# Recurrent stage of a two-layer trunk: three changes of instruction order, and two of eight output tiles finished on VectorE

## What is computed

```
for i in range(2):
    hn = rmsnorm(x, mix_pre_g[i])
    y  = pool_mixer(hn, ...) if i == 0 else mlstm_mixer(hn, ...)
    x  = x + rmsnorm(y, mix_post_g[i])
    hn = rmsnorm(x, ffn_pre_g[i])
    y  = square(relu(hn @ w1[i])) @ w2[i]
    x  = x + rmsnorm(y, ffn_post_g[i])
```

## Time and profile before

| | |
|---|---|
| median of 3 runs | 1971.12 us (1970.82 to 1972.35) |
| the profiled execution's own time | 1969.38 us |
| its span, first to last instruction | 1967.6 us |
| mean granted clock of TensorE | 0.999 |
| PE busy | 1932.8 us, 98% |
| DVE busy | 1321.8 us, 67% |
| ACT busy | 1064.2 us, 54% |
| POOL busy | 91.0 us, 5% |

### The profile page before, as it was taken

The page is one execution under the profiler, slowest core; times in us unless marked ns, Lnnn a source line. Parts: engine busy times, 40 slices in busy tenths (PEclk is TensorE's granted clock), DMA queues, the critical chain, the costliest instruction groups (busy, mean ns, idle before and its releaser), DMA issues. The chain is left out here.

```text
span 1967.6 us, 24435 instructions
## 1 busy us (share of the span) xinstructions
PE 1932.8 (98%) x8582; PEld 1546.2 (79%) x8582; DVE 1321.8 (67%) x2070; ACT 1064.2 (54%) x1803; POOL 91.0 (5%) x121
## 2 busy tenths in 40 slices
PE   9999999999999999999999999899999999999999
PEld 6678888888788788878878878777888888878786
DVE  5775656565678877776866857776656565577864
ACT  7645454554445446766756757544554545445433
POOL 0110000000000100110000100021000000000110
PEclk9999999999999999999999999999999999999999
DMA  5344234348633533343223442243524344853353
GB/s 213 103 157 177 103 136 161 134 177 297 229 94 103 197 111 100 118 150 97 97 77 104 135 135 96 66 150 119 191 91 163 132 165 172 315 186 97 112 196 115
DMA packets 80568, 283.94 MB, mean 144 GB/s; under 512 B 9504, under 2 KB 9632, under 8 KB 73536
## 3 DMA queue, kind: packets, MB, share of 16 engines
q1 hardware_dynamic: 64576, 237.86, 34.6%
q0 software_dynamic: 8320, 27.27, 4.3%
q10 hardware_dynamic: 7552, 17.26, 2.7%
HBM read 213.08 MB, written 69.27 MB: 144 GB/s over the span
## 5 line engine op out<-in xcount | busy, mean ns | idle before, releaser
L1807 DVE TENSOR_TENSOR w_lo<-raw,w_hi 128x1024 fp32r<-128x1024 f32 x148 | 185.8, 1256 | 188.5 <-ACT w_hi L1266 185.4
L1266 ACT CAST w_hi<-raw 128x1024 fp32r<-128x1024 f32 x148 | 154.3, 1042 | 195.7 <-PE core L1006 54.1
L787 PE MATMUL bank<-x_hi,w_hi 128*128 128x512 f32 x560 | 227.4, 406 | 7.0 <-issue 6.6
L1452 ACT CAST h_hi<-h_raw 128x512 fp32r<-128x512 f32 x178 | 110.3, 620 | 222.6 <-PE core L1006 137.5
L789 PE MATMUL bank<-x_hi,w_lo 128*128 128x512 f32 x560 | 221.7, 396 | 0.0
L788 PE MATMUL bank<-x_lo,w_hi 128*128 128x512 f32 x560 | 220.6, 394 | 0.0
L2062 DVE TENSOR_TENSOR h_lo<-h_raw,h_hi 128x512 fp32r<-128x512 f32 x178 | 122.9, 690 | 106.9 <-ACT h_hi L1452 106.5
L1004 PE MATMUL core<-h_hi,w_hi 128*128 128x512 f32 x448 | 177.9, 397 | 2.5 <-ACT w_hi L1468 2.5
L1006 PE MATMUL core<-h_hi,w_lo 128*128 128x512 f32 x448 | 176.8, 395 | 0.0
L1005 PE MATMUL core<-h_lo,w_hi 128*128 128x512 f32 x448 | 176.5, 394 | 0.0
L1956 DVE TENSOR_TENSOR w_lo<-sums,w_hi 128x512 fp32r<-128x512 f32 x96 | 66.3, 691 | 99.7 <-ACT w_hi L1294 97.1
(11 more groups left out here) (333 smaller groups left out, 4444.2 us busy)
## 6 DMA issues: line engine op xcount, KB each, us to landing
raw<-weights SPq DMA_DIRECT2D x148, 512.0 KB, 3.3
h_pair_dram<-y SPq DMA_DIRECT2D x24, 1792.0 KB, 6.6
h_raw<-h_pair_dram SPq DMA_DIRECT2D x168, 256.0 KB, 2.8
w<-second_pairs SPq DMA_DIRECT2D x32, 768.0 KB, 4.5
x_scratch<-y POOLq DMA_DIRECT2D x48, 256.0 KB, 2.6
raw_odd<-first_pairs SPq DMA_DIRECT2D x12, 1024.0 KB, 7.1
raw<-first_pairs SPq DMA_DIRECT2D x12, 1024.0 KB, 7.1
xold<-x_scratch POOLq DMA_DIRECT2D x40, 256.0 KB, 3.8
```

The source lines that it names most:

```text
L787: nc.tensor.matmul(o, a, hi(t), start=(k == 0), stop=False)
L1266: nc.scalar.copy(w_hi[:, ROW[u] * T:(ROW[u] + 2) * T], raw[:, (n % RAW) * BLK:(n % RAW + 1) * BLK]).then_inc(hi_ready, 1)
L1452: nc.scalar.copy(h_slot(n)[0], h_raw[:, at % H_RAW, :]).then_inc(h_hi_ready, 1)
L1807: dve.tensor_tensor(w_lo[:, s], raw[:, (n % RAW) * BLK:(n % RAW + 1) * BLK], w_hi[:, s].bitcast(F32), ALU.subtract).then_inc(lo_ready, 1)
```

## The change

It has four parts.

1. In every round j from 1 to 15, `split_hi` and `split_lo` of the fourth weight block move ahead of `tick(j, 1)`, on ACT and on DVE.
2. In rounds 4, 8 and 12 (`j % FT == 0`) DVE does `gate_head(j-1)` ahead of `tick(j, 2)` and not behind it. In round 8 that tick is empty.
3. After the last head ACT computes `decay_matrix` ahead of `by_tokens`.
4. At the end, tiles 3 and 7 leave PE and ACT: DVE adds the old input itself, directly into the tile that is stored.

```
+END_ADDED = (3, 7)
...
             for k in range(KT):
-                sp.wait_ge(end_taken, k + 1)
+                if k in END_ADDED:
+                    sp.wait_ge(end_added, END_ADDED.index(k) + 1)
+                else:
+                    sp.wait_ge(end_taken, k + 1 - sum(a < k for a in END_ADDED))
                 sp.dma_start(out[1, k], end_sq[:, k, :]).then_inc(out_stored[1], 16)
...
-            for k in range(KT):
-                if k == KT - 1:
-                    pe.wait_ge(std_ready, NORMS)
+            tiles = [k for k in range(KT) if k not in END_ADDED]
+            for k in tiles:
                 nc.tensor.matmul(last_bank(k)[:, :], ident, x_last[:, k, :], start=True, stop=False)
...
                         tick(j - 1, 3)
+                        decay_matrix(j - 1)
                         by_tokens(j - 1)
-                        decay_matrix(j - 1)
...
                         rows_to_all(j)
+                    split_hi(BLOCK["head", j, 2] + 1)
                     tick(j, 1)
-
-                    split_hi(BLOCK["head", j, 2] + 1)
                     conv_input(j, 1)
...
                     states(j - 1)
+                    split_lo(BLOCK["head", j, 2] + 1)
                     tick(j, 1)
-                    split_lo(BLOCK["head", j, 2] + 1)
                     conv(j, 1)
...
+                    if j % FT == 0:
+                        gate_head(j - 1)
                     tick(j, 2)
-                    gate_head(j - 1)
+                    if j % FT:
+                        gate_head(j - 1)
...
+                scaled = normed(dve, y[1][:, k, :], y[1][:, k, :], CHAINS[-1][1] + k)
+                if k not in END_ADDED:
+                    scaled.then_inc(end_scaled, 1)
+                    continue
+                steps.finish(scaled)
+                dve.wait_ge(x_last_landed, 16)
+                dve.tensor_tensor(end_sq[:, k, :], x_last[:, k, :], y[1][:, k, :], ALU.add).then_inc(end_added, 1)
```

More of the change, by code:

```diff
@@ L411, in build @@
         end_taken = sem("last_output_taken")
+        end_added = sem("last_residual_added")
         x_first_landed = sem("first_old_x_landed")
@@ L1177, in _ @@
             pe.wait_ge(y_added, 2 * ADDS)
-            for k in range(KT):
-                if k == KT - 1:
-                    pe.wait_ge(std_ready, NORMS)
+            tiles = [k for k in range(KT) if k not in END_ADDED]
+            for k in tiles:
                 nc.tensor.matmul(last_bank(k)[:, :], ident, x_last[:, k, :], start=True, stop=False)
-            for k in range(KT):
-                pe.wait_ge(end_scaled, k + 1)
+            for at, k in enumerate(tiles):
+                pe.wait_ge(end_scaled, at + 1)
                 nc.tensor.matmul(last_bank(k)[:, :], ident, y[1][:, k, :], start=False, stop=True).then_inc(end_done, 1)
@@ L1789, in _ @@
             root(norms.pop(0))
-            for k in range(KT):
-                act.wait_ge(end_done, k + 1)
+            for at, k in enumerate(k for k in range(KT) if k not in END_ADDED):
+                act.wait_ge(end_done, at + 1)
                 nc.scalar.copy(end_sq[:, k, :], last_bank(k)[:, :]).then_inc(end_taken, 1)
@@ L2424, in _ @@
             for k in range(KT):
-                normed(dve, y[1][:, k, :], y[1][:, k, :], CHAINS[-1][1] + k).then_inc(end_scaled, 1)
+                scaled = normed(dve, y[1][:, k, :], y[1][:, k, :], CHAINS[-1][1] + k)
[5 more added lines that the diff above has]
+                dve.tensor_tensor(end_sq[:, k, :], x_last[:, k, :], y[1][:, k, :], ALU.add).then_inc(end_added, 1)
 def kernel(x, mix_pre_g, mix_post_g, ffn_pre_g, ffn_post_g, pool_w, pool_b, pool_scale,
```

## The result

| | before | changed |
|---|---|---|
| median | 1970.97 us (8 runs, 1969.66 to 1972.35) | 1977.65 us (8 runs, 1976.60 to 1979.53) |
| the profiled execution's own time | 1969.38 | 1976.84 |
| its span | 1967.6 | 1975.0 |
| mean granted clock in it | 0.999 | 0.995 |

The ratio is 1.0036, with a 95% interval of 1.0026 to 1.0046: slower by 6.7 us. The forecast was 1974.5, with 1968.0 to 1977.5 as its range, and no measurable change as its verdict. The median lies 0.15 above the range, and the slowdown is clear.

A forecast was written before the change was run, and what follows sets the result against it. PE, busy 98%, was taken as the bound, waiting on DVE in rounds 2, 4, 10 and 12. 2 x (2.3 + 0.9) + 1.35 + 1.0 - 3.35 - 2.0 = +3.4 took 1971.12 to 1974.5 us; range 1968.0 to 1977.5.

The forecast's parts named there:

- rival B: Fourth blocks: the splits were all that PE waited for; -13.3 us in all, 1957.8; chance 0.07.
- about 3: Sign in rounds 2, 4, 10 and 12: PE idle about 3 us before `turn_back`, no pause at the fourth block.
- a late second block: Round 4, output product: with part 2, PE starts the second block at 877.7, before 876.35; the round costs +1.35.
- A DVE instruction with two SBUF inputs is held until 2.1 us into the reduction: Rule for DVE under POOL's reduction, read from two rows and applied to the convolution in rounds 2 and 10.
- the 2.3 a round: Rounds 2 and 10: convolution held under the reduction until 807.29 for 804.99, +2.3 us in each.
- a held convolution: Rounds 2 and 10: the convolution's three instructions read two SBUF tiles and are held by the reduction, +2.3 us each.
- its bound of 2.5: Rounds 2 and 10: upper bound of part 1's cost, 2.5 us, if the two small copies are held too.
- The step that failed: the clock: Half clock behind PE's pauses: 0.9 us each in rounds 2 and 10, nothing added in rounds 4 and 12.
- rival C: Rounds 2 and 10: the half clock costs its full 1.7; +5.0 us in all, 1976.1; chance 0.24.
- the cover: Rounds 4 and 12: the late second output block covers the lost clock, so the half clock costs nothing there.
- 1.02: Rounds 4 and 12, part 1: the convolution starts 1.02 us later, and `hnorm` and the next `w_lo` with it.
- 1.35: Round 4: cost of parts 1 and 2 together, +1.35 us, through the late second output block; bounds 0 and +2.9.

The follow-up runs named there:

- experiment 13: The full change, with DVE's last state update and two PSUM copies ahead of the convolution in rounds 2 and 10: 1975.6 us, ratio 1.0023.
- Experiment 4: The full change, with PE doing three idle products in its pause before `turn_back` in rounds 2, 4, 10 and 12: 1973.8 us, ratio 1.0018.
- experiment 14: The full change, with PE doing three idle products before `turn_back` in rounds 4 and 12 alone: 1976.4 us, ratio 1.0026.
- experiments 2 and 8: 2: kernel before plus part 1 alone, 1983.5 us; 8: kernel before plus parts 3 and 4, norm-chain work of rounds 2, 4, 10, 12 moved later, 1954.4 us.

## Why the prediction was wrong

**What held.** DVE's work ahead of `hnorm`, not the splits alone, is what PE waits for, so rival B falls: the fourth block lost its pause, and nothing came of it. PE's idle times before `turn_back` are 3.41, 3.41, 3.21 and 3.05, "about 3". Part 2 trades `hid_lo` for a late second block. Part 3 gave 3.4 and part 4 gave 1.9 in the trace. The last head lost its wait:

```profile
1271.93 0.39 PE L1108 MATMUL core<-v_tok,prob 128*128 128x129 f32 x2
```

At the end, ACT's last copy answers to the earlier trace rows:

```profile
1971.26 0.58 ACT L1796 COPY end_sq<-core 128x512 f32<-128x512 f32 x1 [0.27 <-PE core L1189]
```

It stands 10.45 us behind the start of the last reciprocal (1960.81), before 13.01 (1964.53 less 1951.52).

**Right in time, wrong in kind.** "A DVE instruction with two SBUF inputs is held until 2.1 us into the reduction": the 2.1 was right (804.96 + 2.10 - 0.17 - 804.75 = 2.14), and the 2.3 a round with it (2.4 and 2.45). But what was held has one input; it isn't the number of inputs but that all of them lie in SBUF (experiment 13, and the last section). The prediction chose 2.3 for a held convolution; held copies were its bound of 2.5. The Trainium skill, page "SBUF — State Buffer", section "Who interferes with whom", names copies among the instructions that can take the ports shared with GpSimd; the trace agrees, with 2.10 us for 0.17. It also says that whoever issues first keeps them for the whole instruction; the trace agrees for a DVE instruction that starts with the reduction (below), and not for the reduction, which let go at 2.1 of its 3.23 us.

**The step that failed: the clock.** The sum took 0.9 us each in rounds 2 and 10, and nothing in 4 and 12. Experiment 4 measured 3.9 for all four. That is 2.1 of the 3.3 us by which the slowdown (6.7) exceeds the forecast (3.4). By the ledger and experiment 14, in the profiled executions:

- round 2: 1.0 for 0.9, since 1.3 of the 3.4 us lay over the wait for the next block's split.
- round 10: 1.5. The fall came 1.9 us behind the start of `turn_back` and not with it, so that nearly all of it lay on products. The prediction had 1.7 as the bound (rival C) and took half.
- round 4: 0.1, covered. Round 12: 0.85, since the clock was low for 6.8 us and the cover was sized for 3.4.
- the second MLP: 1.5 in the profiled execution, behind a pause of 2.37 us that had been there before without a fall. Of 16 traces it fell in 4, so this is chance and no cost of the change.

**Rounds 4 and 12 without the clock.** Round 12 was sized right: `turn_back` came 1.09 later for 1.02, and with PE kept at work the round costs 1.0, as forecast. In round 4 it came 1.45 later, and the round costs 1.7 for 1.35:

```profile
865.48 0.69 DVE L1888 TENSOR_TENSOR y<-xold,step_t 128x512 f32<-128x512 f32 x1
866.66 0.17 DVE L2205 COPY craw<-taps 128x16 f32<-128x16 f32 x1 [0.50 <-DVE y L1888]
```

DVE waits 0.50 behind its own residual before it goes on. At the same two instructions it waits 0.14 in round 12, and 0.14 in 23 of the 28 places where they meet in the 16 traces; the other five, of 0.50, are round 4 in five of the traces. Why there is not shown.

**In medians.** Predicted and measured: parts 3 and 4 -5.35 and -5.1, rounds 2 and 10 6.4 and 7.6, rounds 4 and 12 2.35 and 3.2. These add to 5.7, and the full change measured 6.7. The last 1.0 is open. It is less than the intervals can tell, since each ratio is known to about 0.001, or 2 us. The runs of the full change had a clock of 0.993 to 0.995, where the parts' add up to 0.995, so one more half-clock stretch in most runs would do, but no run here isolates it.

## What to carry to other kernels

When an engine pauses, ask which instruction of its supplier comes last in that round, and move work out from ahead of that one: swapping two things that both stand ahead of it only moves the pause (experiments 2 and 8). Price a new pause of TensorE twice, as a wait and as half-clock products behind it, and, for a pause of 3 us or more, give the second its upper bound unless a later wait longer than what two such stretches cost stands there. Before moving an instruction past the start of a POOL reduction, look at what it puts under it: something that reads PSUM was not held there in any trace, something within SBUF was.

## What the runs showed of the hardware

**The clock is a matter of chance for middling pauses.** In the 16 traces (before, changed, 14 experiments), at all 19 pauses of PE of 3.0 us or more the clock fell, from 1.2 us before PE resumed to 2.0 us after; it did so at 16 of 37 between 2.1 and 2.9, and at none of 117 between 1.0 and 1.9. The same pause of 2.19, in code that is the same in all 16 kernels and ends at about 67 us, fell in 7 of 16 executions, the 2.14 at the last head in 4 of 4, the 2.37 of the second MLP in 4 of 16. The half-clock stretches lasted 3.41 or 6.83 us, those that begin after PE's last product left out.

**It explains most of the scatter.** In the experiments' comparison runs the kernel before took 1969.3 us on average with a mean clock of 0.999 (23 runs), 1970.4 with 0.998 (41), and 1971.8 with 0.997 (26). Within each kernel the slope is 1.3 us for each 0.001, and it takes up 0.8 of the variance.

**The reduction and DVE.** Whether the reduction holds a DVE instruction could have been read for both kinds of input before the change. DVE and POOL of the kernel before, in round 5:

```profile
907.28 0.35 DVE L2236 SCALAR_TENSOR_TENSOR mid<-state,inter_b,core 128x129 f32<-128x129 f32 x1 [0.50 <-PE core L1091]
907.67 0.73 DVE L2236 SCALAR_TENSOR_TENSOR mid<-mid,inter_b,core 128x129 f32<-128x129 f32 x2
908.44 1.82 DVE L1807 TENSOR_TENSOR w_lo<-raw,w_hi 128x1024 fp32r<-128x1024 f32 x1
```

```profile
906.93 3.23 POOL L1229 PARTITION_ALL_REDUCE tot<-acc  x1 [33.57 <-DVEq L1876]
```

The three `mid`, which read `core` in PSUM, take their usual 0.35 under the reduction; the split behind them, within SBUF, takes 1.82 for 1.23. The 16 traces have 230 DVE instructions that started once a reduction was running and over 1.2 us before its end. None of the 101 with an input in PSUM was held, and 128 of the 129 with all inputs in SBUF were (the other one stood behind a DVE instruction that had begun before the reduction). All of them write SBUF. The held ones began to work 1.13 or 1.14 us before the reduction ended: 2.1 us into one of 3.23, and 3.2 us into one of 4.31.

A reduction that starts in the same moment as a DVE split leaves the split alone and takes 1.08 us longer itself than the 3.23 of the others. POOL and DVE of the changed kernel:

```profile
1306.47 4.31 POOL L1234 PARTITION_ALL_REDUCE tot<-acc  x1 [105.94 <-DVEq L1880]
```

```profile
1306.47 1.23 DVE L1811 TENSOR_TENSOR w_lo<-raw,w_hi 128x1024 fp32r<-128x1024 f32 x1
```
